# One step of a hybrid decoder on one core: the experts' weight fetches cut into runs of 2 and 4 KB, and the next block's rows copied behind the sigmoids

## The chip, the cores and the metric

The kernel runs on one NeuronCore of a Trainium2 chip. TensorE (PE) multiplies matrices, VectorE (DVE) and ScalarE (ACT) work on tiles, GpSimd (POOL) and SyncE (SP) issue most transfers, and 16 DMA engines move the bytes. The metric is the device time of one execution in microseconds (us), given as the median of several runs.

## What is computed

One layer for 2048 prompt tokens and 32 sample tokens: a modulated norm, one input projection, stick-breaking attention beside a gated linear recurrence, an output projection, and then a mixture of 32 experts, of which each token uses two. The last part is the one that matters here:

```python
def routed_experts(x, expert_idx, gate, w1, w3, w2):
    # pairs (token, expert) are sorted by expert into blocks, each block belonging to one expert
    def expert_block(args):
        toks, e = args
        xb = x_pad[toks]
        hb = jax.nn.silu(xb @ w1[e]) * (xb @ w3[e])
        return hb @ w2[e]
    out = lax.map(expert_block, (row_tok.reshape(n_blocks, EXPERT_BLOCK), block_expert))
    ...
```

w1 and w3 are 1024 x 512 and w2 is 512 x 1024, all float32, so an expert has three matrices of 2 MB. The token rows are 1024 numbers wide.

## The kernel before

The phases follow each other: modulation, projections, attention, the output projection with the router, the experts, and a final phase that gathers the experts' results, adds them and normalises. The change is in the experts (`experts_of`), with the matching layouts elsewhere.

The router writes each token row into `xs_d0` and `xs_d1` in memory, sorted by expert. The experts' phase then works through blocks of 64 rows; an expert has at least one block, and its number of blocks is read at run time (`n_blocks`), so that every engine runs a loop over an expert's blocks, 32 loops after each other. In this trace there are 80 blocks; by the times of the fetches of SP most experts have 2 or 3, and some have 1 or 4. A block has two units (u = 0, 1) of 32 rows.

Its steps, each on one engine, with the lines of the kernel:

- POOL (`load`, L1935) issues four transfers of 64 KB for the rows of a block into `x_in` (the profile shows `rowsP<-xs_d`), a double buffer, waits until they have landed, then issues two stores of 128 KB (`store`, L1944, `ys_d<-y`) of the result of two blocks earlier, and goes on with the next block's load. Both go by the software queue q0.
- ACT (`landed`, L1965) waits for the rows of block n + 1 and copies them into `x_turn` (shown as `o_rs<-rowsP`). It then does the sigmoids of block n (`gated`, L1970, `sg<-bank`), one for each unit, and last copies block n's result out of its bank (`result`, L1975, `y<-bank`).
- DVE multiplies the sigmoid with both products (L2033, L2035) and transposes the outcome into `hT` (L2037), for one unit; then it turns that unit of the next block's rows, `x_turn` into `xT` (`turn_rows`, L2028, shown as `o_sq<-o_rs`); then the same for the other unit.
- PE does the first products of both units (`hidden`, L1993, 64 matmuls each), which need `xT` and the expert's w1 and w3, and then the second products (`out`, L2000, 32 each), which need `hT` and w2. `xT` and the banks `h` have one buffer for each unit.
- SP fetches the weights by the hardware queue q1 into three slots: w1 and w3 of an expert (L1908) when the last block of the expert three before it has finished `hidden`, and w2 (L1916) when it has finished `out`. A transfer of 2 MB is laid out so that each of the 128 partitions gets one run of 16 KB.

The slots are memory of earlier phases (`oT`, `w_out`, `w`), which is why the profile shows the fetches as `oT<-in_w`, `w_out<-in_w` and `w<-in_w`. Waits are counted semaphores. On each engine instructions run in the order written.

Of the kernel before, what the change touches and what calls it, by code (L numbers as in the profile page):

```python
# [15 lines left out]
P = 128  # L16
D = 1024
KC = D // P
# [15 lines left out]
DE = D // 2  # L34
EC = DE // P
G = 64
STRIPS = 4
Q = P // STRIPS
UNITS = G // Q
# [806 lines left out]
def attention_phase(nc, io, keep, sems):  # L846
# [20 lines left out]
    for n in range(TICKS):  # L867
        unit, p = place(n)
# [15 lines left out]

    with ExitStack() as stack:
        k = Kit(nc, stack)
        shared = keep["w13_0"][:, :, :, :].rearrange("p a c n -> p (a c n)")
        kT = [shared[:, SEQ * i:SEQ * i + SEQ] for i in range(2)]
        qT = [shared[:, SEQ * (2 + i):SEQ * (2 + i) + SEQ] for i in range(2)]
        vv = [k.sb(f"vv{i}", [P, NT, P]) for i in range(2)]  # L890
# [532 lines left out]
def router(nc, io, keep, sems, k):  # L1423
# [59 lines left out]
    def sync(sp):  # L1483
        sp.dma_start(nf_row[:, :], io["norm_ffn"].to_broadcast([P, D])).then_inc(s["small"], 16)

        def load_x(i):
            if i == 0:
                sp.dma_start(x_t[0][0:NS, :], io["x_sample"].rearrange("b t n -> (b t) n")).then_inc(s_x[0], 16)
            else:
                sp.dma_start(x_t[i % 2][:, :], x_src[i - 1]).then_inc(s_x[i % 2], 16)  # L1490

        def load_rg(i):
            sp.dma_start(featT[i % 2][:, FC:, :], rgT[i - 1]).then_inc(s_rg[i % 2], 16)

        load_rg(1)
        load_x(0)
        sp.dma_start(w_r[:, :, 0:NG], io["w_group"][0].rearrange("(c p) n -> p c n", p=P)).then_inc(s["wr"], 16)
        sp.dma_start(w_r[:, :, 8:RW], io["w_router"][0].rearrange("(c p) n -> p c n", p=P)).then_inc(s["wr"], 16)
        sp.dma_start(b_r[:, 0:NG], io["b_group"].to_broadcast([P, NG])).then_inc(s["small"], 16)
        sp.dma_start(b_r[:, 8:RW], io["b_router"].to_broadcast([P, NE])).then_inc(s["small"], 16)  # L1500
        load_x(1)
        load_rg(2)
        for at, name in enumerate(("w1", "w3")):
            sp.dma_start(keep["w13_0"][:, at, :, :], io[name][0, 0].rearrange("(p c) n -> p c n", p=P)).then_inc(sems["pre"], 16)
        for i in range(NTL):
            sp.wait_ge(s["x1"], i + 1)
            sp.dma_start(io["x1_d"][row0[i]:row0[i] + size[i], :], x1[i % 2][0:size[i], :]).then_inc(s_st[i % 2], 16)
            if i + 2 < NTL:
                load_x(i + 2)
            if i >= 1 and i + 2 < NTL:  # L1510
                sp.wait_ge(s["mm1"], i + 1)
                load_rg(i + 2)
        for b in range(2):
            sp.wait_ge(s_st[b], 16 * len(range(b, NTL, 2)))
# [336 lines left out]
def experts_of(nc, io, keep, sems, k, emptied):  # L1851
# [37 lines left out]
    def sync(sp):  # L1889
        done = sp.alloc_register("blocks_done")  # L1890
        sp.reg_mov(done, 0)
        emptied(sp, "low")
        sp.dma_start(w2[0][:, :, :], src["w2"][0].rearrange("(p j) n -> p j n", p=P)).then_inc(s_w2[0], 16)
        sp.wait_ge(sems["placed"], 1)
        sp.wait_ge(s["in"], 64)
        for e in range(NE):
            i = e % SLOTS
            if e == 1:
                emptied(sp, "oT")
            if e == 2:  # L1900
                emptied(sp, "w_out")
            if e >= SLOTS:
                sp.reg_add(done, done, blocks_of(sp, e - SLOTS))
                freed = sp.snap(done, min_val=1, max_val=MAX_BLOCKS)
                hold(sp, s["h1"], freed, s["sp"])
            if e > 0:
                for at, name in enumerate(("w1", "w3")):
                    sp.dma_start(w13[i][:, at, :, :], src[name][e].rearrange("(p c) n -> p c n", p=P)).then_inc(s_w13[i], 16)  # L1908
            if e == 1:
                emptied(sp, "mid")  # L1910
            if e == 2:
                emptied(sp, "high")
            if e >= SLOTS:
                hold(sp, s["y"], freed, s["sp"])
            if e > 0:
                sp.dma_start(w2[i][:, :, :], src["w2"][e].rearrange("(p j) n -> p j n", p=P)).then_inc(s_w2[i], 16)  # L1916
        x1_rows = io["x1_d"][0:SEQ, :].rearrange("(t p) n -> p t n", p=P)
        sp.reg_add(done, done, blocks_of(sp, NE - 3))
        hold(sp, s["y"], sp.snap(done, min_val=1, max_val=MAX_BLOCKS), s["sp"])
        sp.dma_start(keep["x1_a"], x1_rows[:, 0:8, :]).then_inc(sems["x1_a"], 16)  # L1920
        sp.dma_start(keep["x1_b"], x1_rows[:, 8:12, :]).then_inc(sems["x1_b"], 16)
        sp.reg_add(done, done, blocks_of(sp, NE - 2))
        hold(sp, s["y"], sp.snap(done, min_val=1, max_val=MAX_BLOCKS), s["sp"])
        sp.dma_start(keep["x1_c"], x1_rows[:, 12:16, :]).then_inc(sems["x1_c"], 16)
        sp.dma_start(keep["x1_s"], io["x1_d"][SEQ:, :]).then_inc(sems["x1_s"], 16)
# [34 lines left out]
    def scalar(act):  # L1960
        def landed(n):

            act.wait_ge(s["in"], 64 * n + 64)
            act.wait_ge(s["xT"], 2 * n + 1)
            act.activation(x_turn[:, :].rearrange("p (u c a) -> p u c a", u=UNITS, c=KC),  # L1965
                           x_in[:, ds(n & 1, 1), :].rearrange("p z (u a c) -> p (z u) c a", u=UNITS, c=KC), ACT.Copy).then_inc(s["cp"], 1)

        def gated(n, u):
            act.wait_ge(s[f"h{u}"], n + 1)
            act.activation(sg[:, u, :], h[u][:, 0:P], ACT.Sigmoid).then_inc(s["sg"], 1)  # L1970

        def result(n):
            act.wait_ge(s["st"], 32 * n + 64)
            act.wait_ge(s["y"], n + 1)
            act.activation(y[:, ds(n & 1, 1), :].rearrange("p a n -> p (a n)"), yb[:, :], ACT.Copy).then_inc(s["ye"], 1)  # L1975

        def body(n, e, b, extra):
            landed(n + 1)
            for u in range(UNITS):
                gated(n, u)  # L1980
            result(n)

        act.nop().then_inc(s["xT"], 1)
        act.wait_ge(sems["placed"], 1)
        landed(0)
        experts(act, body)

    def tensor(pe):
        def hidden(i, u):

            for c in range(KC):
                for q in range(STRIPS):
                    mm = pe.matmul(h[u][q * Q:q * Q + Q, 0:2 * P], xT[:, c, u, :], w13[i][:, :, c, q * P:q * P + P], start=(c == 0), stop=(c == KC - 1))  # L1993
            return mm

        def out(i, u):

            for j in range(EC):
                for q in range(STRIPS):
                    mm = pe.matmul(yb[q * Q:q * Q + Q, u * (XW // 2):(u + 1) * (XW // 2)], hT[:, u, j, :], w2[i][:, j, q * (XW // 2):(q + 1) * (XW // 2)],  # L2000
                                   start=(j == 0), stop=(j == EC - 1))
            return mm

        def body(n, e, b, extra):
            i = e % SLOTS
            for u in range(UNITS):
                pe.wait_ge(s["xT"], 2 * n + u + 2)
                hidden(i, u).then_inc(s[f"h{u}"], 1)
            pe.wait_ge(s_w2[i], 16 * (e // SLOTS) + 16)
            for u in range(UNITS):  # L2010
                pe.wait_ge(s["hT"], 2 * n + u + 1)
                mm = out(i, u)
            mm.then_inc(s["y"], 1)

        def before(e):
            i = e % SLOTS
            if e == 0:
                pe.wait_ge(sems["pre"], 32)
            else:
                pe.wait_ge(s_w13[i], 32 * (e // SLOTS + (1 if i else 0)))  # L2020

        pe.wait_ge(sems["placed"], 1)
        experts(pe, body, before)

    def vector(dve):
# [4 lines left out]
        def body(n, e, b, extra):  # L2030
            for u in range(UNITS):
# [3 lines left out]
                dve.tensor_tensor(hid[:, u, :], sg[:, u, :], h[u][:, P:2 * P], ALU.mult)  # L2035
                dve.drain()
                dve.transpose(hT[:, u, :, :].rearrange("p j b -> p (j b)"), hid[:, u, :].rearrange("p (a j) -> p j a", j=EC)).then_inc(s["hT"], 1)  # L2037
                turn_rows(n + 1, u)

        for u in range(UNITS):  # L2040
# [158 lines left out]
def build_program(nc, io):  # L2199
    with ExitStack() as stack:  # L2200
# [35 lines left out]
        keep["rowsP"] = k.sb("rowsP", [P, 4, D])  # L2236
        rows_s = k.sb("rowsS", [P, 4, D])
        keep["rowsS"], keep["rows_mem"] = rows_s[0:NS, :, :], (keep["rowsP"], rows_s)
        keep["w13_0"] = k.sb("w13_0", [P, 2, KC, DE])
        keep["oT"], keep["w_out"] = k.sb("oT", [P, FC, SEQ]), k.sb("w_out", [P, 2, KC, 512])  # L2240
        for name in ("w_out0", "w_out1", "rows", "x1_a", "x1_b", "x1_c", "x1_s"):
            sems[name] = k.sem(name)
        attention_phase(nc, io, keep, sems)
        for i in range(3):
            keep[f"w2_{i}"] = k.sb(f"w2_{i}", [P, EC, D])
        keep["w13_1"] = keep["oT"][:, :, :].rearrange("p f n -> p (f n)").rearrange("p (a c n) -> p a c n", c=KC, a=2)
        keep["w13_2"] = keep["w_out"][:, :, :, :]
        tiles = lambda t: t[:, :, :, :].rearrange("p a c n -> p (a c n)").rearrange("p (t d) -> p t d", d=D)
        keep["x1_a"], keep["x1_b"] = tiles(keep["w13_2"]), keep["w2_2"][:, :, :]
        keep["x1_c"], keep["x1_s"] = tiles(keep["w13_0"])[:, 0:4, :], tiles(keep["w13_0"])[0:NS, 4, :]  # L2250
        keep["yy"] = tiles(keep["w13_1"])
# [35 lines left out]
```

## Time and profile before

| | |
|---|---|
| median of 3 runs | 3134.55 us (3132.65 to 3138.47) |
| the profiled execution, its own time | 3157.24 us |
| its span in the trace | 3155.8 us |
| PE busy | 2642.2 us, 84% of the span |
| DVE busy | 1365.3 us, 43% |
| ACT busy | 1051.0 us, 33% |
| POOL busy | 647.3 us, 21% |

Busy time counts the spans of instructions. In the experts' phase, from the first `hidden` at 1846.5 us to the end of the last `out` at 3058.9 us, PE is busy for less of the time than elsewhere. The profile page cuts the span into 40 slices of 79 us; the experts lie in slices 24 to 39. A row of the cost list gives the line, the engine, what it writes and reads and the shapes, how often, then busy time, the mean of one, and the idle time of the engine just before such instructions with what ended it.

### The profile page before, as it was taken

To read this page: it belongs to the slowest core of one execution; us is meant where nothing else is said; L and a number is where in the kernel's file an instruction comes from. 1 tells how busy PE (TensorE), PEld (TensorE's weight loads), DVE (VectorE), ACT (ScalarE), POOL (GpSimd) and SP (SyncE) were. 2 spreads that over 40 slices of the span, in tenths; PEclk is the share of its full clock that TensorE was granted. 3 is DMA by queue.
4 is the path that set the end of the run, shared out by engine and by line. 5 is a ranking of instruction groups with operands and counts; after the bars stand their busy time and mean duration, and the time that the engine had idled before them with its cause. 6 is when DMAs were issued, how large, how long until landed. Compare 5 with 4: busy or idle time off the path is not lost. (4 is left out here: it accounts for less than half of the span.)

```text
span 3155.8 us, 63798 instructions
## 1 busy us (share of the span) xinstructions
PE 2642.2 (84%) x23589; PEld 1368.9 (43%) x23589; DVE 1365.3 (43%) x2816; ACT 1051.0 (33%) x1942; POOL 647.3 (21%) x914
## 2 busy tenths in 40 slices
PE   7999999968898989999999927977678846777777
PEld 3444444424454444454355514544344423443443
DVE  2141424237787878888677721211111111111118
ACT  2313030216777777777222112111111111111114
POOL 0101010110121111111022222322232212222233
PEclk8999999988999999999999959988899878898889
DMA  8020201175776776767434365566455587656537
GB/s 300 13 80 15 78 27 67 49 258 179 264 252 225 238 235 228 247 223 240 157 126 144 120 244 194 191 208 240 152 198 174 165 294 245 237 156 246 186 107 305
DMA packets 225280, 576.76 MB, mean 183 GB/s; under 512 B 78230, under 2 KB 94679, under 8 KB 208780
## 3 DMA queue, kind: packets, MB, share of 16 engines
q1 hardware_dynamic: 123304, 427.99, 37.7%
q0 software_dynamic: 101440, 145.99, 15.4%
q8 instruction: 115, 1.88, 0.2%
q14 instruction: 97, 0.79, 0.1%
q10 hardware_dynamic: 324, 0.10, 0.0%
HBM read 460.86 MB, written 112.29 MB: 182 GB/s over the span
## 5 line engine op out<-in xcount | busy, mean ns | idle before, releaser
L2000 PE MATMUL bank<-w,hT 128*32 128x256 f32 x5120 | 348.2, 431 | 315.2 <-DVE hT L2037 315.2
L2033 DVE TENSOR_TENSOR sg<-sg,bank 128x128 f32<-128x128 f32 x160 | 44.6, 279 | 978.9 <-ACT sg L1970 978.7
L1253 DVE TENSOR_TENSOR_SCAN left<-leave,left 128x512 f32<-128x512 f32 (+3 forms) x320 | 358.4, 1120 | 135.9 <-ACT leave L1135 135.3
L2000 PEld LDWEIGHTS bank<-w,hT 128*32 128x32 f32 x5120 | 173.0, 124 | 483.3 <-DVE hT L2037 347.9
L442 PE MATMUL bank<-xnT,w_in 128*128 128x512 f32 x768 | 330.3, 592 | 0.0
L1944 POOL DMA_DIRECT2D ys_d<-y x164 | 115.9, 712 | 810.0 <-issue 743.6
L1056 POOL DMA_DIRECT2D w_out<-in_cache_v x256 | 137.8, 538 | 661.2 <-issue 656.0
L1965 ACT ACTIVATE o_rs<-rowsP 128x512 f32 (+1 forms) x81 | 92.9, 1146 | 464.6 <-DMA rowsP<-xs_d 454.2
L1935 POOL DMA_DIRECT2D rowsP<-xs_d x324 | 215.1, 672 | 85.1 <-issue 84.2
L1993 PE MATMUL bank<-w,o_sq 128*32 128x256 f32 x3840 | 214.7, 382 | 20.0 <-DVE o_sq L2028 20.0
L1620 PE MATMUL bank<-w_out,w 128*128 128x512 f32 x512 | 229.4, 601 | 2.5 <-DVE w L1684 2.5
L442 PEld LDWEIGHTS bank<-xnT,w_in 128*128 128x128 f32 x768 | 145.6, 190 | 181.8 <-issue 178.9
L442 PE MATMUL bank<-w_in,xnT 128*128 128x512 f32 x512 | 220.4, 592 | 0.0
L1137 ACT ACTIVATE take<-zb,biasP 128x512 f32<-128x512 f32 (+3 forms) x320 | 207.2, 647 | 0.0
L1135 ACT ACTIVATE leave<-zb,nbiasP 128x512 f32<-128x512 f32 (+3 forms) x320 | 204.5, 639 | 8.0 <-PE zb L1297 8.0
L1304 PE MATMUL tb<-ident,take 128*128 128x128 f32 x1088 | 182.4, 285 | 28.8 <-DVE take L1159 25.1
L1993 PE MATMUL bank<-oT,o_sq 128*32 128x256 f32 x3712 | 205.6, 379 | 0.5 <-issue 0.5
L1159 DVE TENSOR_TENSOR take<-take,left 128x512 f32<-128x512 f32 (+3 forms) x320 | 194.7, 609 | 15.5 <-DVE left L1253 0.4
L1291 PE MATMUL zb<-w 64*128 64x512 f32 (+3 forms) x640 | 164.3, 591 | 30.5 <-ACT take L1137 19.4
L1304 PEld LDWEIGHTS tb<-ident,take 128*128 128x128 f32 x1088 | 120.4, 143 | 147.0 <-issue 79.0
L1339 PE MATMUL tb<-ident,w_out 128*128 128x128 f32 x1024 | 160.7, 281 | 27.4 <-DMA w_out<-in_cache_k 22.4
L1975 ACT ACTIVATE y<-bank 128x512 f32 x80 | 47.8, 597 | 387.2 <-PE bank L2000 337.4
(409 smaller groups left out, 3424.9 us busy)
## 6 DMA issues: line engine op xcount, KB each, us to landing
w<-in_w SPq DMA_DIRECT2D x54, 2048.0 KB, 15.9
w_out<-in_cache_v POOLq DMA_DIRECT2D x256, 256.0 KB
w_out<-in_cache_k SPq DMA_DIRECT2D x256, 256.0 KB
oT<-in_w SPq DMA_DIRECT2D x22, 2048.0 KB, 14.1
w_out<-in_w SPq DMA_DIRECT2D x20, 2048.0 KB, 14.4
ys_d<-zeros SPq DMA_DIRECT2D x32, 816.0 KB
ys_d<-y POOLq DMA_DIRECT2D x166, 128.0 KB, 4.8
rowsP<-xs_d POOLq DMA_DIRECT2D x324, 64.0 KB, 4.0
```

The source lines that it names most:

```text
L442: mm = pe.matmul(ps[:, :], w, m, start=(i == 0), stop=(i == len(parts) - 1))
L1135: act.activation(leave[n % 4][:, 0:cols], zb[n % 3][:, 0:cols], ACT.Sigmoid, scale=-SCALE, bias=keep["nbiasP"][:, head:head + 1]).then_inc ...
L1137: act.activation(take[n % 4][:, 0:cols], zb[n % 3][:, 0:cols], ACT.Sigmoid, scale=SCALE, bias=keep["biasP"][:, head:head + 1]).then_inc(s_ ...
L1159: dve.tensor_tensor(take[n % 4][:, 0:cols], take[n % 4][:, 0:cols], left[n % 4][:, 1:cols + 1], ALU.mult).then_inc(s_w, 1)
L1253: dve.tensor_tensor_scan(left[n % 4][:, 0:cols][:, ::-1], leave[n % 4][:, 0:cols][:, ::-1], leave[n % 4][:, 0:cols][:, ::-1], left[n % 4][ ...
L1291: mm = pe.matmul(zb[(n + par) % 3][:, 0:cols], qT[pair % 2][half, t * P:t * P + P], kT[pair % 2][half, c * GRP:c * GRP + cols], start=True ...
L1304: mm = pe.transpose(to[:, j * P:j * P + P], take[n % 4][:, j * P:j * P + P], ident[:, :])
L1339: mm = pe.transpose(to[:, i * P:i * P + P], kp[g % 2][:, i, f * P:f * P + P], ident[:, :])
L1620: mm = pe.matmul(pb[half][0:n, :], lhs, w_out[:, half, c, :], start=(c == 0), stop=(c == KC - 1))
L1935: pool.dma_start(x_in[64 * half:64 * half + 64, ds(n & 1, 1), u * (XW // 2):(u + 1) * (XW // 2)].rearrange("p a n -> p (a n)"), in_strips( ...
L1993: mm = pe.matmul(h[u][q * Q:q * Q + Q, 0:2 * P], xT[:, c, u, :], w13[i][:, :, c, q * P:q * P + P], start=(c == 0), stop=(c == KC - 1))
L2000: mm = pe.matmul(yb[q * Q:q * Q + Q, u * (XW // 2):(u + 1) * (XW // 2)], hT[:, u, j, :], w2[i][:, j, q * (XW // 2):(q + 1) * (XW // 2)], s ...
```

## The change

The layout of the w1/w3 slots goes from [w1 or w3, c, n] to [c, w1 or w3, n], c being the 8 rows of the matrix that a partition holds. The transfer of one matrix therefore writes 8 runs of 2 KB into a partition, in place of one of 16 KB; in memory it is still 16 KB in one piece. PE reads the two halves of its operand 2 KB apart in place of 16 KB. The fetch of w2 is cut into four transfers, one for each j, with 4 KB for each partition, and the wait of PE counts four times as much. On ACT the wait for the next block's rows and their copy come after both sigmoids. On DVE both units' products come first, and then both turns.

```diff
@@ experts, sync
-                    sp.dma_start(w13[i][:, at, :, :], src[name][e].rearrange("(p c) n -> p c n", p=P)).then_inc(s_w13[i], 16)
+                    sp.dma_start(w13[i][:, :, at, :], src[name][e].rearrange("(p c) n -> p c n", p=P)).then_inc(s_w13[i], 16)
...
-                sp.dma_start(w2[i][:, :, :], src["w2"][e].rearrange("(p j) n -> p j n", p=P)).then_inc(s_w2[i], 16)
+                for j in range(EC):
+                    sp.dma_start(w2[i][:, j, :], src["w2"][e].rearrange("(p j) n -> j p n", p=P)[j]).then_inc(s_w2[i], 16)
@@ experts, scalar
         def body(n, e, b, extra):
-            landed(n + 1)
             for u in range(UNITS):
                 gated(n, u)
+            landed(n + 1)
             result(n)
@@ experts, tensor
-                    mm = pe.matmul(h[u][q * Q:q * Q + Q, 0:2 * P], xT[:, c, u, :], w13[i][:, :, c, q * P:q * P + P], start=(c == 0), stop=(c == KC - 1))
+                    mm = pe.matmul(h[u][q * Q:q * Q + Q, 0:2 * P], xT[:, c, u, :], w13[i][:, c, :, q * P:q * P + P], start=(c == 0), stop=(c == KC - 1))
...
-            pe.wait_ge(s_w2[i], 16 * (e // SLOTS) + 16)
+            pe.wait_ge(s_w2[i], 16 * EC * (e // SLOTS + 1))
@@ experts, vector
                 dve.transpose(hT[:, u, :, :].rearrange("p j b -> p (j b)"), hid[:, u, :].rearrange("p (a j) -> p j a", j=EC)).then_inc(s["hT"], 1)
+            for u in range(UNITS):
                 turn_rows(n + 1, u)
```

The first expert's w1 and w3, fetched in the router's phase (L1504), and its w2 (L1893) are cut in the same way, and the views of this memory in the attention and the final phase are renamed to match, at the same addresses.

On ScalarE, in the loop of the second expert, one block is this before (`o_rs<-rowsP` is the copy of the next block's rows, `sg` the two sigmoids, `y` the result; an ISA row is a wait or a count):

```order
L1884 ISA
L1964 ISA
L1965 REGISTER_ALU
L1965 ISA
L1965 ACTIVATE o_rs<-rowsP 128x512
L1970 ACTIVATE sg<-bank_4 128x128
L1970 ACTIVATE sg<-bank_6 128x128
L1973 ISA
L1975 REGISTER_ALU
L1975 ISA
L1975 ACTIVATE y<-bank_3 128x512
```

and this with the change:

```order
L1884 ISA
L1972 ACTIVATE sg<-bank_4 128x128
L1972 ACTIVATE sg<-bank_6 128x128
L1965 ISA
L1966 ISA
L1967 REGISTER_ALU
L1967 ISA
L1967 ACTIVATE o_rs<-rowsP 128x512
L1975 ISA
L1977 REGISTER_ALU
L1977 ISA
L1977 ACTIVATE y<-bank_3 128x512
```

The copy and its two waits stand behind both sigmoids now, and still ahead of the result.

On VectorE one block of the first expert is this before (`hT` feeds PE's second products, `o_sq` is one unit of the next block's rows turned):

```order
L2033 TENSOR_TENSOR sg<-sg,bank_4 128x128
L2035 TENSOR_TENSOR hid<-sg,bank_4 128x128
L2037 STREAM_TRANSPOSE hT<-hid 128x128
L2027 REGISTER_ALU
L2028 STREAM_TRANSPOSE o_sq<-o_rs 128x8x32
L2032 REGISTER_ALU
L2033 TENSOR_TENSOR sg<-sg,bank_6 128x128
L2035 TENSOR_TENSOR hid<-sg,bank_6 128x128
L2037 STREAM_TRANSPOSE hT<-hid 128x128
L2028 STREAM_TRANSPOSE o_sq<-o_rs 128x8x32
```

and this with the change:

```order
L2035 TENSOR_TENSOR sg<-sg,bank_4 128x128
L2037 TENSOR_TENSOR hid<-sg,bank_4 128x128
L2039 STREAM_TRANSPOSE hT<-hid 128x128
L2034 REGISTER_ALU
L2035 TENSOR_TENSOR sg<-sg,bank_6 128x128
L2037 TENSOR_TENSOR hid<-sg,bank_6 128x128
L2039 STREAM_TRANSPOSE hT<-hid 128x128
L2029 REGISTER_ALU
L2030 STREAM_TRANSPOSE o_sq<-o_rs 128x8x32 x2
```

The first turn moved behind the second unit's `hT`, and both turns stand together at the end of the block.

On SyncE the fetches of one later expert are this before (w1 and w3, then w2):

```order
L1874 TENSOR_LOAD n_blocks
L1874 ISA x2
L1903 ISA
L1908 DMA w_0<-in_w 128x4096 x2
L1916 DMA w_0<-in_w 128x4096
```

and this with the change:

```order
L1874 TENSOR_LOAD n_blocks
L1874 ISA x2
L1904 ISA
L1909 DMA w_0<-in_w 128x8x512 x2
L1918 DMA w_0<-in_w 128x1024 x4
```

The order of the fetches is the same; w2 has four instructions in place of one.

## Rows read from the trace of the kernel before

**Rows 1.** The experts' whole phase: start:end, its length, each engine's busy time.

```profile
1846.50:3058.90 1212.40, 896.36 (x15360) 498.39 (x15360) 206.49 (x641) 184.43 (x328) 326.29 (x482) 0.87 0.60 204
```

**Rows 2.** The page's cost list: the experts' instructions, busy, mean ns, idle before.

```profile
L2000 PE MATMUL bank<-w,hT 128*32 128x256 f32 x5120 | 348.2, 431 | 315.2 <-DVE hT L2037 315.2
L1965 ACT ACTIVATE o_rs<-rowsP 128x512 f32 (+1 forms) x81 | 92.9, 1146 | 464.6 <-DMA rowsP<-xs_d 454.2
```

**Rows 3.** Who waited for whom from 1900 us on: us in total, times, longest.

```profile
PE bank L2000 <- DVE hT L2037: 281.8, 37, 24.5
```

**Rows 4.** Timeline of ACT, PE, POOL and SP around one weight fetch.

```profile
2257.70 1.12 ACT L1965 ACTIVATE o_rs<-rowsP 128x512 f32 x1 [18.11 <-DMA rowsP<-xs_d]
2258.72 0.43 ACT L1970 ACTIVATE sg<-bank 128x128 f32<-128x128 f32 x2
...
2238.52 7.09 PE L1993 MATMUL bank<-oT,o_sq 128*32 128x256 f32 x128
...
2234.66 2.65 POOL L1935 DMA_DIRECT2D rowsP<-xs_d  x4 [0.52 <-issue]
2258.50 1.41 POOL L1944 DMA_DIRECT2D ys_d<-y  x2 [21.19 <-issue]
...
2235.32 0.81 SPq L1908 DMA_DIRECT2D w<-in_w  x2
2238.83 0.33 SPq L1916 DMA_DIRECT2D w<-in_w  x1
```

**Rows 5.** Timeline of PE, ACT, POOL and DVE in blocks with no fetch running.

```profile
2265.41 7.08 PE L1993 MATMUL bank<-oT,o_sq 128*32 128x256 f32 x128
2272.32 3.69 PE L2000 MATMUL bank<-w,hT 128*32 128x256 f32 x64
2275.82 7.09 PE L1993 MATMUL bank<-oT,o_sq 128*32 128x256 f32 x128
...
2277.13 1.16 ACT L1965 ACTIVATE o_rs<-rowsP 128x512 f32 x1 [0.23 <-DMA rowsP<-xs_d]
2282.98 0.28 ACT L1970 ACTIVATE sg<-bank 128x128 f32<-128x128 f32 x1 [3.17 <-PE bank L1993]
...
2270.20 2.65 POOL L1935 DMA_DIRECT2D rowsP<-xs_d  x4 [0.52 <-issue]
...
2284.01 0.42 DVE L2037 STREAM_TRANSPOSE hT<-hid 128x128 f32<-128x128 f32 x1
2284.36 0.40 DVE L2028 STREAM_TRANSPOSE o_sq<-o_rs 128x256 f32<-128x256 f32 x1
```

**Rows 6.** DMA packets by queue: a fetch running (2240:2252), none (2266:2292), attention (848:856).

```profile
q1 hardware_dynamic: 296, 4.33, 95.7%
q0 software_dynamic: 287, 0.14, 4.4%
...
q0 software_dynamic: 1959, 1.27, 21.6%
...
q0 software_dynamic: 463, 1.51, 51.6%
q1 hardware_dynamic: 762, 1.40, 47.8%
```

**Rows 7.** Stretches with 2 KB runs alone (35:50) and weight fetches; last: DMA share, GB/s.

```profile
35.00:40.00 5.00, 3.02 (x20) 1.64 (x12) 2.08 (x5) 0.00 (x0) 0.00 (x0) 0.50 1.05 387
...
2300.00:2306.00 6.00, 3.77 (x75) 2.00 (x68) 1.06 (x4) 1.46 (x3) 1.41 (x2) 1.00 1.02 419
...
2244.00:2250.00 6.00, 1.61 (x32) 0.70 (x24) 0.00 (x0) 0.00 (x0) 0.00 (x0) 1.00 1.02 362
```

**Rows 8.** Issue durations of SP's 2 MB transfers in 2 KB runs: ns min/median/max.

```profile
L152 SPq DMA_DIRECT2D w_in<-in_w_in x3: 1183/5021/21543, 7.3 to 30.1; - x3
```

**Rows 9.** SP's fetches where experts have a single block each.

```profile
2578.03 0.81 SPq L1908 DMA_DIRECT2D w<-in_w  x2
...
2614.23 1.08 SPq L1908 DMA_DIRECT2D oT<-in_w  x2
```

More of the change, by code:

```diff
@@ L886, in attention_phase @@
         k = Kit(nc, stack)
-        shared = keep["w13_0"][:, :, :, :].rearrange("p a c n -> p (a c n)")
+        shared = keep["w13_0"][:, :, :, :].rearrange("p c a n -> p (c a n)")
         kT = [shared[:, SEQ * i:SEQ * i + SEQ] for i in range(2)]
@@ L1503, in sync @@
         for at, name in enumerate(("w1", "w3")):
-            sp.dma_start(keep["w13_0"][:, at, :, :], io[name][0, 0].rearrange("(p c) n -> p c n", p=P)).then_inc(sems["pre"], 16)
+            sp.dma_start(keep["w13_0"][:, :, at, :], io[name][0, 0].rearrange("(p c) n -> p c n", p=P)).then_inc(sems["pre"], 16)
         for i in range(NTL):
@@ L1892, in sync @@
         emptied(sp, "low")
-        sp.dma_start(w2[0][:, :, :], src["w2"][0].rearrange("(p j) n -> p j n", p=P)).then_inc(s_w2[0], 16)
+        for j in range(EC):
+            sp.dma_start(w2[0][:, j, :], src["w2"][0].rearrange("(p j) n -> j p n", p=P)[j]).then_inc(s_w2[0], 16)
         sp.wait_ge(sems["placed"], 1)
@@ L1915, in sync @@
             if e > 0:
-                sp.dma_start(w2[i][:, :, :], src["w2"][e].rearrange("(p j) n -> p j n", p=P)).then_inc(s_w2[i], 16)
+                for j in range(EC):
+                    sp.dma_start(w2[i][:, j, :], src["w2"][e].rearrange("(p j) n -> j p n", p=P)[j]).then_inc(s_w2[i], 16)
         x1_rows = io["x1_d"][0:SEQ, :].rearrange("(t p) n -> p t n", p=P)
@@ L2238, in build_program @@
         keep["rowsS"], keep["rows_mem"] = rows_s[0:NS, :, :], (keep["rowsP"], rows_s)
-        keep["w13_0"] = k.sb("w13_0", [P, 2, KC, DE])
+        keep["w13_0"] = k.sb("w13_0", [P, KC, 2, DE])
         keep["oT"], keep["w_out"] = k.sb("oT", [P, FC, SEQ]), k.sb("w_out", [P, 2, KC, 512])
@@ L2245, in build_program @@
             keep[f"w2_{i}"] = k.sb(f"w2_{i}", [P, EC, D])
-        keep["w13_1"] = keep["oT"][:, :, :].rearrange("p f n -> p (f n)").rearrange("p (a c n) -> p a c n", c=KC, a=2)
-        keep["w13_2"] = keep["w_out"][:, :, :, :]
-        tiles = lambda t: t[:, :, :, :].rearrange("p a c n -> p (a c n)").rearrange("p (t d) -> p t d", d=D)
+        keep["w13_1"] = keep["oT"][:, :, :].rearrange("p f n -> p (f n)").rearrange("p (c a n) -> p c a n", c=KC, a=2)
+        keep["w13_2"] = keep["w_out"][:, :, :, :].rearrange("p h c n -> p (h c n)").rearrange("p (c a n) -> p c a n", c=KC, a=2)
+        tiles = lambda t: t[:, :, :, :].rearrange("p c a n -> p c (a n)")
         keep["x1_a"], keep["x1_b"] = tiles(keep["w13_2"]), keep["w2_2"][:, :, :]
```

## The prediction

> **What bounds the kernel now.** The window over the experts' phase comes first, since every edit lies there: 1212.4 us, in which PE is busy for 896 us at a granted clock of 0.87, with the DMA engines at 0.60 [rows 1]. So neither is full. The cost list then says what PE waits for: its second products (L2000) stand idle for 315.2 us, all of it on `hT` from DVE, and take 348.2 us themselves [rows 2]. The list of waits counts 37 such waits from 1900 us on, up to 24.5 us long [rows 3]. In the same list ACT's copy of the next block's rows idles for 464.6 us until the rows have landed [rows 2].
>
> The timeline around one fetch joins the two [rows 4]. SP issues w1 and w3 at 2235.3 and w2 at 2238.8. POOL issues the rows of the next block at 2234.7 to 2237.3, and ACT can copy them only at 2257.7. PE ended its first products at 2245.6, and both sigmoids, which need nothing but these, run at 2258.7, because they stand behind the copy. In blocks with no fetch running PE never stops: first products from 2265.41 and again from 2275.82, a period of 10.42 us; the copy starts 1.3 us after the start of a block and is done before the first of PE's two units is ready, half of 7.09 us in [rows 5]. So the bound is a chain: **rows held behind weights, then sigmoids held behind rows, then PE**. 80 blocks (5120 matmuls of 64 each, [rows 2]) at 10.42 us are 834 us; the other 378 us are this chain and its cold clock: 315.2 us idle, and 348.2 - 80 x 3.69 = 53 us of second products that run slow after a halt [rows 2, 5].
>
> **The change: the runs of 2 and 4 KB.** The turn behind a weight packet shrinks. 2 KB runs alone moved 387 GB/s over 16 engines, so one takes 2.048 x 16 / 387 = 0.085 us [rows 7]; a 4 KB one is twice that, 0.17 us. How many go by in one turn is not shown for these two transfers. The nearest row is the attention phase, K in 2 KB runs on q1 beside V in 4 KB packets on q0: 762 packets to 463, 1.65 to one, about equal bytes [rows 6]. So a block's 49 packets cost 49 x 0.085 = 4.2 us at one run a turn, 6.9 us at 1.65, 8.3 us beside w2. Without a fetch, the loads go from the start of issue (2270.20) to the copy (2277.13) in 6.9 us, of which 2.65 is issuing and most is latency; the packets run beside that [rows 5]. I add to the landing, inside a fetch: 0.5 us at the best, 5 us at the worst (all turns of 4 KB and none beside the issuing), and take **2.9 us**, nearest to the attention row.
>
> The Trainium skill (DMA: Bandwidth & Descriptors, SWDGE vs HWDGE vs iDMA) calls a packet the point at which an engine switches queues, and prefers at most 4096 B for one. Turns of 4 KB would be 0.17 us for both matrices, the upper half of my range; the 14.6 KB mean of [rows 6] shows that packets are larger where a run is.
>
> The fetch itself hardly slows: 387 GB/s against 362 to 419 with 16 KB runs [rows 7], 6.29 MB in 16.3 us. SP's issue of a 2 KB-run transfer can block for 1.2 to 21.5 us [rows 8]; behind it on SP stand only the later fetches (and the loads of x1 at the end), in their order anyway, so I cost it at nothing; were the DMA engines idle meanwhile, it would be the rival on weights below. Three more issues for w2 at 0.33 us each [rows 4] lie on SP too. PE's operand with halves 2 KB apart has no row of its own; the matmuls run the same from all slots, so nothing.
>
> **The change: the order.** In the block above PE can do its second products (3.69 us, with 1.2 us of DVE's steps ahead, 2283.26 to 2284.43 [rows 5]) while it waits for the rows. Before, rows had to land within 2.5 us of a block's start to hold nobody (the copy of 1.16 us must end when the first unit does, at 3.6 us). With the change they must land 2.0 us before the next block (copy 1.16, turn 0.40, steps between), at 8.4 us. They land at 1.1 to 1.3 us [rows 5], so slack grows from 1.3 to about 7 us. The late turns cost nothing: the second sigmoid is at 2282.98, 7.2 us into its block, the copy then ends at 8.4, DVE's products by 8.6, both turns by 9.5, and PE needs them at 10.42 [rows 5]. If they were late, each block would pay the difference, 1 us for 80.
>
> **What is late next: POOL's own loop.** It loads, waits for the landing, stores, loads. Copy at 2257.70 (rows landed just before), the next issue 2.7 us later (stores 0.8 us after the copy's start, 1.41 us long, 0.52 us to the next issue [rows 4]), 2.65 issuing, about 4 to land: 9.4 us a turn, only 1 us less than PE's 10.42. Inside a fetch it is 9.4 + 2.9 = 12.3 us. 32 fetches of 16.3 us are 522 us, 59% of a phase near 890 us. Mean turn 9.4 + 0.59 x 2.9 = **11.1 us**, above 10.42: the rows' loop sets the pace, by a little. Then 80 x 11.1 = 888, and 2.5 us for the cold first block: 891 us against 1212.4, a gain of 321. From the profiled 3157.2 that leaves 2836; that execution stands 22.7 us over the median of 3134.55, so I forecast **2813 us**.
>
> Its ends: if the extra landing is 0.5 us, PE sets the pace, 80 x 10.42 + 2.5 = 836, gain 376, 2758 us. If it is 5 us, the loop is 9.4 + 0.55 x 5 = 12.2, the phase 975, gain 237, 2897 us.
>
> **The rivals.** *Rows still wait for the whole fetch.* The DMA engines might take turns by more than one short run, or join the runs of w1 and w3, whose 16 KB stand in one piece in memory. Against it stands the 1.65 to one of attention [rows 6]. Then only the order helps: the 37 waits [rows 3] lose up to 4.9 us each, I take 4, 148 us, and the fetches are longer by some 0.6 us, 20 in all: 3157 - 128 - 22.7 = 3006 us. By the Trainium skill (DMA: Bandwidth & Descriptors, Queues, rings and completion order) an engine drains a whole packet of typically 9 to 17 descriptors before it switches rings. With 2 KB runs that would be a turn as long as before or longer, and this rival; rows 6 show 1.65 in attention, not 9. Chance 12%.
>
> *PE waits for weights.* At the faster pace an expert of one block gives 10.4 us for a fetch of 16.3; fetches at 2578.0 and 2614.2 follow one block each [rows 9]. Three slots cover two such in a row. Should 2 KB runs beside rows move only 240 GB/s, a fetch takes 26 us, and four or five short experts cost 15 us each, with other small gaps: about 100 us more, 2915 us. Attention's window, 2.91 MB in 8 us on both queues, 364 GB/s, speaks against it [rows 6]. Chance 8%.
>
> *Slower.* The same mechanism, worse: SP's blocked issues [rows 8] let q1 run dry between runs. It decides from where a fetch takes longer than an expert does now, 1212.4 / 32 = 37.9 us, that is under 166 GB/s. At 150 GB/s, 41.9 us and 1341 us in all, 3263 us. 387 GB/s behind blocked issues at 35 us speaks against it [rows 7]. Chance 3%.
>
> **The numbers.** Forecast 75% (2758 to 2897), rows still held 12% (2960 to 3050), weights 8% (2880 to 3100), slower 3%, no change 2%. The range 2755 to 2940 holds the first and half the weights' case, 8 in 10. A difference under 0.2% can't be told from none here. Faster 0.95, same 0.02, slower 0.03.
>
> **What would show it.** Right: idle of L2000 on `hT` falls from 315 us to under 30, L2000's mean from 431 to about 380 ns, the clock above 0.95; what idle is left stands before L1993, on `o_sq` from DVE, behind ACT's copy behind the rows; the rows' longest landing falls from beyond 20 us to near 10; q1's packets rise by some 70,000. Wrong: ACT's copy still starts at the end of fetches (the first rival); PE's first products idle on a transfer of `in_w` (the second); fewer GB/s while a fetch runs alone (the third).

## The result, and the profile after

| | before | changed |
|---|---|---|
| median | 3134.84 us (3132.65 to 3138.47, 4 runs) | 3005.06 us (3003.26 to 3017.72, 4 runs) |
| ratio to before | | 0.9594, 95% interval 0.9566 to 0.9621 |
| span of the profiled execution | 3155.8 us | 3001.8 us |
| experts' phase | 1212.4 us | 1060.7 us |

The kernel is faster by 130 us, where 321 were forecast and at least 195 within the range. All of the gain is in the experts' phase: from the end of the last `out` to the end of the kernel it is 97 us in both. The phase is shorter by 152 us and not by 130, because the profiled execution of the kernel before ran 22 us over its median and that of the changed kernel 2 us under; all readings of the traces below carry this. The window over the phase, to be held against [rows 1]:

```profile
1844.50:2905.20 1060.70, 900.43 (x15360) 500.21 (x15360) 221.66 (x641) 184.12 (x323) 325.49 (x482) 0.93 0.77 233
```

PE's wait has changed its place. The cost list of the changed kernel, against [rows 2] (the second products are L2002 here, the first L1995, by the slot they read):

```profile
L1995 PE MATMUL bank<-w,o_sq 128*32 128x256 f32 x3840 | 238.9, 412 | 86.8 <-DVE o_sq L2030 86.8
L2002 PE MATMUL bank<-w,hT 128*32 128x256 f32 x5120 | 295.8, 381 | 0.0
L1995 PE MATMUL bank<-oT,o_sq 128*32 128x256 f32 x3712 | 221.8, 400 | 48.0 <-DVE o_sq L2030 45.5
L1995 PE MATMUL bank<-w_out,o_sq 128*32 128x256 f32 x2688 | 164.4, 407 | 45.2 <-DVE o_sq L2030 43.8
```

The idle of 315.2 us ahead of the second products is gone, and 86.8 + 48.0 + 45.2 = 180 us stand ahead of the first ones, on the turned rows. The cold clock went there with it: second products run at 381 ns, and the first ones take 625 us in place of 80 x 7.09 = 567. Around one such halt, of 3.8 us in the timeline below, the granted clock (PEclk, the third number from the end) is 1.00 before it and 0.60 behind it:

```profile
2238.00:2242.00 4.00, 3.97 (x75) 1.98 (x64) 1.00 (x3) 0.28 (x1) 0.00 (x0) 1.00 1.10 262
2245.70:2250.00 4.30, 4.26 (x48) 2.29 (x52) 0.31 (x1) 0.00 (x0) 2.24 (x4) 0.60 1.01 389
```

So the phase would be 834 + 180 + 58 = 1072 us; it is 1060.7, as parts of these overlap. The waits beneath, from 1890 us on:

```profile
ACT o_rs L1967 <- DMA rowsP<-xs_d: 217.0, 49, 9.1
PE bank L1995 <- DVE o_sq L2030: 149.3, 38, 7.6
```

So ACT still waits for rows, 49 times, but never for more than 9.1 us. The timeline around one fetch shows how late, POOL first, then ACT, PE and SP:

```profile
2230.85 2.65 POOL L1937 DMA_DIRECT2D rowsP<-xs_d  x4 [0.55 <-issue]
2244.89 1.41 POOL L1946 DMA_DIRECT2D ys_d<-y  x2 [11.40 <-issue]
...
2238.52 0.28 ACT L1972 ACTIVATE sg<-bank 128x128 f32<-128x128 f32 x1 [3.18 <-PE bank L1995]
2244.09 1.12 ACT L1967 ACTIVATE o_rs<-rowsP 128x512 f32 x1 [5.29 <-DMA rowsP<-xs_d]
...
2238.27 3.70 PE L2002 MATMUL bank<-w,hT 128*32 128x256 f32 x64
2245.74 4.48 PE L1995 MATMUL bank<-w_out,o_sq 128*32 128x256 f32 x48 [3.77 <-DVE o_sq L2030]
...
2228.16 1.29 SPq L1909 DMA_DIRECT2D oT<-in_w  x2
2231.67 6.12 SPq L1918 DMA_DIRECT2D w<-in_w  x4
```

The fetch starts at 2228.2, and its last piece lands at 2253.0. The rows issued at 2230.8 are copied at 2244.1, 13.2 us later and well before the fetch is over; in [rows 4] it took 23.0 us, the whole fetch. SP's four issues of w2 take 6.1 us, held one after the other.

**The mean turn of POOL's loop** tells all the kernels of this study apart. A load is the time from the first of a block's row transfers' issue to the last one's landing; the gap is the time from there to the next block's issue. Both are means over the 80 blocks, worked out from the issues and landings in the traces (the profile's own rows show single transfers, so that these means have no row).

| | load | of them over 10 us | gap | load + gap | phase / 80 |
|---|---|---|---|---|---|
| before | 11.3 us | 35, mean 17.3 | 3.8 us | 15.1 us | 15.2 us |
| changed | 9.5 | 36, mean 13.1 | 3.7 | 13.2 | 13.3 |
| short runs alone | 10.0 | 44, mean 12.5 | 3.7 | 13.6 | 13.7 |
| new order alone | 12.0 | 29, mean 21.9 | 3.7 | 15.7 | 15.7 |
| rows in wide transfers | 8.6 | 33, mean 11.5 | 3.5 | 12.1 | 12.3 |
| stores issued ahead | 10.4 | 50, mean 12.5 | 2.0 | 12.4 | 12.5 |

In every one of them the phase is 80 turns of this loop, to within 0.2 us a turn. That alone proves nothing, since any loop that keeps step with the blocks has this length. What shows that this one sets the pace is that POOL waits in it for nothing but its own landings. When nothing else holds it, its first store follows the landing by 1.07 us. In the changed kernel that is so, to 0.15 us, in 78 of 80 turns, and all 80 lose 1 us together on anything else; in the kernel before it is 68 of 80, and 7.5 us together. **So POOL's loop set the pace already in the kernel before**, and PE's 315 us on `hT` were what it left idle. The gap's 3.7 us are 1.07 us, 1.41 us of stores (more in some turns) and 0.5 to 0.6 us to the next load; in 31 turns, as many as there are changes of expert, that last step takes 1.1 us more.

### The profile page after: what moved, and what is told of

It is laid out like the page before. It is cut to its first block and busy times, and to the rows that moved or that the text cites. A ratio compares the mean times of both kernels' runs of the same rounds, so it can differ in the third digit from the quotient of the medians.

```text
span 3001.8 us, 63970 instructions
## 1 busy us (share of the span) xinstructions
PE 2644.7 (88%) x23589; PEld 1370.9 (46%) x23589; DVE 1380.3 (46%) x2816; ACT 1051.2 (35%) x1938; POOL 647.7 (22%) x914
## 3 DMA queue, kind: packets, MB, share of 16 engines
q0 software_dynamic: 101440, 145.99, 16.0%
## 5 line engine op out<-in xcount | busy, mean ns | idle before, releaser
L1995 PE MATMUL bank<-w,o_sq 128*32 128x256 f32 x3840 | 238.9, 412 | 86.8 <-DVE o_sq L2030 86.8
L2002 PE MATMUL bank<-w,hT 128*32 128x256 f32 x5120 | 295.8, 381 | 0.0
L1995 PE MATMUL bank<-oT,o_sq 128*32 128x256 f32 x3712 | 221.8, 400 | 48.0 <-DVE o_sq L2030 45.5
L1972 ACT ACTIVATE sg<-bank 128x128 f32<-128x128 f32 x160 | 44.4, 278 | 567.7 <-PE bank L1995 567.7
L1995 PEld LDWEIGHTS bank<-w,o_sq 128*32 128x32 f32 x3840 | 129.6, 119 | 193.6 <-DVE o_sq L2030 95.1
L2002 PEld LDWEIGHTS bank<-w,hT 128*32 128x32 f32 x5120 | 157.1, 110 | 124.2 <-DVE hT L2039 26.8
L1995 PE MATMUL bank<-w_out,o_sq 128*32 128x256 f32 x2688 | 164.4, 407 | 45.2 <-DVE o_sq L2030 43.8
L1995 PEld LDWEIGHTS bank<-oT,o_sq 128*32 128x32 f32 x3712 | 123.4, 115 | 144.0 <-DVE o_sq L2030 52.3
## 6 DMA issues: line engine op xcount, KB each, us to landing
w<-in_w SPq DMA_DIRECT2D x128, 512.0 KB, 15.1
```

## The experiments

Experiments 1 to 4, 5 to 8 and 9 to 12 ran in three groups, each beside executions of the kernel before, with medians of 3139.9, 3131.9 and 3140.0 us; the changed kernel's own comparison had 3134.8. Ratios are to these. A difference in us between kernels of different groups is good to some 8 us, and where it matters, the one by the ratios stands beside it.

**1. The short runs alone**: the changed kernel with ACT's and DVE's order of before.

```diff
         def body(n, e, b, extra):
+            landed(n + 1)
             for u in range(UNITS):
                 gated(n, u)
-            landed(n + 1)
             result(n)
```

> The short runs alone, with the order of the kernel before: the copy still stands ahead of both sigmoids. The theory now (the turns of the rows' packets were priced too low: beside 2 KB runs a block's rows take about 13 us from issue to landing in place of the 8 to 10 forecast, so that POOL's loop of load, landing, store makes about 16 us inside a fetch): that loop sets the pace whatever ACT's order is, so 3005 to 3050 us, with the rows' longest landing near 13 us. The first rival of the prediction (only the order helps, the rows still wait for the whole fetch): 3135 to 3155 us and landings of 20 us and more.

Measured: 3047.7 us, ratio 0.9702 (0.9639 to 0.9766), the longest landing of a row transfer 14.5 us. The loop holds, and the first rival of the prediction, by which the short runs change nothing for the rows, is out. The time lies at the upper end of the first range. The idle time is back at its old place, 189.6 us:

```profile
L2002 PE MATMUL bank<-w,hT 128*32 128x256 f32 x5120 | 354.4, 438 | 189.6 <-DVE hT L2039 189.6
```

**2. The new order alone**: the kernel before, with the diff's lines on ACT and DVE and nothing else.

> The new order on ACT and DVE alone, with runs of 16 KB. The prediction priced this at 3134.8 - 148 = 2987 us, fetches staying as they are. The theory now expects the same, 2980 to 3010 us, with rows landing only at the end of a fetch (over 20 us) and PE's waits moved from the second products to the first. If the short runs carry the gain and the order nothing, 3110 to 3135 us.

Measured: 3202.5 us, ratio 1.0175 (1.0115 to 1.0236), slower than before by 1.2 to 2.4%. It lies in neither range: the prediction's price for the order and the theory as it stood both failed. The timeline of this kernel, POOL, SP and PE:

```profile
2220.75 2.64 POOL L1935 DMA_DIRECT2D rowsP<-xs_d  x4 [0.63 <-issue]
...
2255.05 2.65 POOL L1935 DMA_DIRECT2D rowsP<-xs_d  x4 [0.52 <-issue]
...
2218.57 0.81 SPq L1908 DMA_DIRECT2D w_out<-in_w  x2
...
2252.65 0.80 SPq L1908 DMA_DIRECT2D w<-in_w  x2
...
2228.69 3.69 PE L2000 MATMUL bank<-w,hT 128*32 128x256 f32 x64
2242.80 9.72 PE L1993 MATMUL bank<-w,o_sq 128*32 128x256 f32 x128 [10.42 <-DVE o_sq L2028]
```

POOL's load of 2220.75 stands behind the fetch of 2218.57, and PE waits for it until 2242.80. It has done its second products during the wait, as it should. But SP asks for the next weights as soon as the first products that follow are done (2242.80 + 9.72 = 2252.52), at 2252.65, and POOL's load of 2255.05 falls right behind that and waits for the whole fetch. In the old order PE has its second products still to do when the rows land, some 5 us, and the request comes that much later. The traces bear this out over the 29 fetches of w1 and w3 for which they have both landings. In the new order the next load is issued 0.6 to 4.4 us behind 26 of them, and takes 18.9 to 33.9 us. In the kernel before only 4 have a load that close behind; 19 have one 0.3 to 3.1 us ahead, and 12 of these 19 loads landed in under 20 us, the shortest in 10.4. Loads of over 20 us number 20 here and 11 before. The idle time ahead of the first products is 371 us:

```profile
L1993 PE MATMUL bank<-w,o_sq 128*32 128x256 f32 x3840 | 235.8, 408 | 148.9 <-DVE o_sq L2028 148.0
L1993 PE MATMUL bank<-oT,o_sq 128*32 128x256 f32 x3712 | 228.8, 409 | 113.3 <-DVE o_sq L2028 113.3
L1993 PE MATMUL bank<-w_out,o_sq 128*32 128x256 f32 x2688 | 170.1, 417 | 109.1 <-DVE o_sq L2028 108.9
```

**3. Fewer packets for the rows**: the changed kernel, with whole rows in one array.

```diff
                 for u in range(UNITS):
-                for half in range(2):
-                    pool.dma_start(x_in[64 * half:64 * half + 64, ...], in_strips(io[f"xs_d{half}"], row, u))
+                pool.dma_start(x_in[:, ...], in_strips(io["xs_d"], row, u))
```

> The changed kernel, with the two arrays of half rows made one array of whole rows (room for 2048 rows for each expert), so that a block's rows come in two transfers of 128 partitions and 128 KB in place of four of 64 partitions and 64 KB, as the stores of results do, which show no 16-byte packets. The theory (40 of a block's 49 packets for each engine are 16-byte ones, each takes a turn of about 0.16 us beside the fetch): if the tiny packets go with the 64-partition form, a load lands within 8 us inside a fetch, PE sets the pace again and the time is 2790 to 2850 us. If the tiny packets stay, 2980 to 3010 us. If bytes and not packets hold the rows, no change, 2990 to 3010 us with the tiny packets gone.

Measured: 2929.9 us, ratio 0.9319 (0.9263 to 0.9374), between the cases. The tiny packets did not go, and the premise was wrong: stores have them too. Two stores stand alone in 3050 to 3060 us of the kernel before, with 64 packets of 4 KB for their 256 KB, and 224 under 512 B:

```profile
q0 software_dynamic: 288, 0.27, 11.8%
```

By size the trace has 192 packets of 16 B among them, 96 for each store, and 32 of 4 B. Over the whole kernel that leaves 112 for each load of 64 KB and, in this experiment, 96 for each load of 128 KB. A block has 54 packets on each engine, 36 of its loads and 18 of its stores; with the wide transfers the loads too have 18. So q0's packets fall by a quarter (the changed kernel has 101440):

```profile
q0 software_dynamic: 77568, 145.64, 16.0%
```

The bytes are the same, and inside a fetch a load takes 11.5 us in place of 13.1. Most of that is not the contention, though: with no fetch beside it a load takes 5.3 us in place of 6.3, since POOL issues two transfers in place of four (1.4 us in place of 2.65). What a fetch adds falls only from 6.8 to 6.2 us, with the loads' packets halved. The mean turn falls by 1.1 us, and the fewer issues alone take 1.0 off a quiet load. At a fixed 0.16 us a packet, 18 fewer on each engine would have taken 2.9 us off a load inside a fetch; so the packets do not set the landing alone.

**4. The stores out of the loop**: the changed kernel, in which POOL issues a block's loads, then the stores, and then waits for the landing.

```diff
-            hold(pool, s["in"], 64 * n + 64, s["sp"])
...
             store(n)
+            hold(pool, s["in"], 64 * n + 64, s["sp"])
```

> The changed kernel, but POOL issues the stores of an earlier result right behind a block's loads and waits for their landing only then, so that the stores no longer lie between a landing and the next issue. The theory (POOL's loop sets the pace): a turn inside a fetch falls from about 16 to about 13.5 us, 60 of 80 blocks gain some 2 us, 2870 to 2930 us. If PE or the weights set the pace: no change, 3000 us.

Measured: 2942.4 us, ratio 0.9355 (0.9298 to 0.9411). That is a gain, but 12 us short of the range. The gap fell by 1.7 us; loads rose by 0.9, which the expectation had left out (the stores' packets may now run among theirs). This is a gain of 63 us over the changed kernel (75 by the ratios) by an edit that touches no transfer, and the plainest sign that the loop sets the pace.

**5. No fetches**: experts 4 to 32 use the weights of the first three.

> The changed kernel without the fetches of the 4th to the 32nd expert: these compute with the weights of the first three. It leaves 29 x 6.29 MB of transfers out and shows the phase with nothing beside the rows. The theory (rows lose time only to the fetch; quiet, a load takes 6.3 us and the next issue 3.7 more, under PE's 10.42): the experts' phase takes 80 x 10.42 and some 15 us for the start, about 850 us, and the whole 2785 to 2805 us. If POOL's loop is the bound even when quiet, 2830 us and more.

Measured: 2803.9 us, one run, phase 859 us. This is the floor of PE's pace. Quiet, load and gap are 6.3 + 3.7 = 10.0 us, just under PE's 10.42. Here POOL does wait for others: its first store follows the landing by over 1.2 us in 36 of 80 turns, 23 us together.

**6. w2 by one transfer** of 16 KB runs, the rest as changed.

> The changed kernel with w2 fetched by one transfer of 16 KB runs again; w1 and w3 keep 2 KB. The theory (one turn of the rows' queue is one run of the weights' queue): rows that meet the w2 part of a fetch, 8 turns of 0.65 us for each engine in place of 32 of some 0.2 us, land later by 3 to 5 us; with one block in two to three meeting it, 3040 to 3110 us. If the runs of w2 don't matter, 2995 to 3015 us.

Measured: 3010.3 us, ratio 0.9594 (0.9553 to 0.9636). No difference from the changed kernel, against the expectation. Loads of the rows are asked for right after w1 and w3 and meet those. The expectation had taken the fetch for evenly spread over the rows. The cut of w2 is worth nothing here.

**7. Runs of 1 KB** for w1 and w3.

> The changed kernel with w1 and w3 in runs of 1 KB (w2 stays at 4 KB). In the changed kernel a turn of a rows' packet beside 2 KB runs takes 0.16 us. If about 0.085 of it is the run and the rest is fixed, a turn falls to 0.11 to 0.12 us, a load inside a fetch from 13.1 to about 11 us, and half the blocks gain 2 us: 2900 to 2960 us. If the turn is a cost of the rows' own packet, whatever stands beside it, landings stay at 13 us, fetches get longer, and the time is 3005 to 3050 us.

Measured: 2993.6 us, ratio 0.9552 (0.9511 to 0.9594), some 11 us under the changed kernel, so neither case in full; the intervals of the two ratios touch, and the phase in the traces is 10 us shorter (1050.7 us). Packets by queue in a stretch where rows and weights share the engines, first the changed kernel (2236 to 2240 us), then this one (2229 to 2233):

```profile
q1 hardware_dynamic: 403, 0.80, 81.0%
q0 software_dynamic: 402, 0.27, 29.2%
```

```profile
q1 hardware_dynamic: 617, 0.62, 86.1%
q0 software_dynamic: 450, 0.19, 36.4%
```

402 packets of the rows in 4 us on 16 engines are one in 0.159 us; with 1 KB runs 450 are one in 0.142 us. Halving the run takes 0.017 us off the turn, not 0.04. But it is no longer one run a turn: 617 to 450 is 1.37, so that a turn still carries 1.4 KB of weights. By estimate from 0.085 us for 2 KB, the runs' part of a turn falls from 0.085 to 0.058 us, and the rest, 0.074 and 0.084 us, stays. In the kernel before a turn was 12 x 16 / 287 = 0.67 us [rows 6].

**8. Wide rows and stores ahead together**, on the changed kernel.

> Rows in two transfers of 128 partitions (room for 2048 rows for each expert) and the stores of results issued ahead of the wait for the landing, both on the changed kernel. Alone they gave loads of 8.6 us and 3.5 us to the next issue, and 10.4 and 2.0 us. The theory (the phase is 80 turns of POOL's loop, a turn being load and gap, with PE's 10.42 below it): 8.6 + 1.0 for the later stores + 1.8 = 11.4 us, 912 us of phase, 2855 to 2885 us. If the gains overlap, 2915 to 2930 us.

Measured: 2833.6 us (2832.3 to 2836.5), ratio 0.9039 (0.9004 to 0.9075), 21 us under the range and 30 us above the run without fetches. Loads 8.7, gap 2.4, 11.1 us a turn, and a phase of 895 us, 11.2 a block. For the first time something else shows beside the loop, 16 us on the weights:

```profile
L1994 PE MATMUL bank<-w,o_sq 128*32 128x256 f32 x3840 | 215.8, 383 | 34.7 <-DVE o_sq L2029 25.1 <-DMA w<-in_w 9.5
L1994 PE MATMUL bank<-w_out,o_sq 128*32 128x256 f32 x2688 | 153.6, 387 | 14.8 <-DVE o_sq L2029 7.9 <-DMA w_out<-in_w 6.2 <-issue 0.8
```

This version gives each expert room for 2048 rows less the first 64, which is enough for these inputs and not for every routing. Experiment 4 has no such limit.

**9 and 10. What each half of the change is worth once the loop is fast.** Number 9 is number 8 with runs of 16 KB, number 10 is number 8 with the old order.

> The kernel of e8_wide_ahead (rows in two wide transfers, room for 2048 rows for each expert, stores ahead of the wait) with the weights in runs of 16 KB again, in the new order. The theory: a load's 36 packets for each engine are still more than a fetch's 24, so rows are held for whole fetches, about 20 us, and only the shorter gap (2.3 in place of 3.7 us) and quiet load (5.3 in place of 6.3 us) help: a loop of 13 to 13.8 us, 2960 to 3040 us. If the short runs owe their gain only to the slow loop, it is within 1% of e8's 2833.6 us.

> The kernel of e8_wide_ahead with ACT's and DVE's order of the kernel before (the copy ahead of both sigmoids). The theory: where POOL's loop no longer sets the pace, the slack that the new order gives (about 6 us a block) is what hides a late load; without it each load that lands over 2.5 us into its block is paid at once. 27 loads over 10 us, 2 to 3 us each: 2880 to 2930 us. If the order is worth nothing here either, 2830 to 2845 us.

Measured: 2980.9 us (ratio 0.9478, 0.9430 to 0.9526) and 2876.8 us (0.9150, 0.9103 to 0.9196). The first is in its range, the second 3 us under it. So the runs are worth 147 us there (138 by the ratios), and the order 43 us (35 by the ratios). In number 10 the idle is ahead of the second products again:

```profile
L2001 PE MATMUL bank<-w,hT 128*32 128x256 f32 x5120 | 306.1, 392 | 67.4 <-DVE hT L2038 67.1
```

**11. Runs of 1 KB on number 8.**

> The kernel of e8_wide_ahead with w1 and w3 in runs of 1 KB. On the changed kernel this gave 11 us (loads inside a fetch 11.8 in place of 13.1 us, fetches slower). Here little is left above the floor of 2804 us: 2820 to 2835 us. If the slower fetch makes PE wait for weights, 2840 to 2870 us with idle of PE's first products on transfers of in_w.

Measured: 2842.8 us, ratio 0.9039 (0.8992 to 0.9087), the same as number 8 within the intervals. The time lies in the second case, and its sign came too: PE's idle on transfers of `in_w` is 24 us in place of 16. Finer runs have nothing left to give.

**12. Rows from a fixed address**, to see where the 16-byte packets come from.

```diff
-            load(n, pool.snap(e * CAP + offs + b * G))
+            load(n, e * CAP)
```

> The changed kernel with each block's rows read from a fixed place of its expert's room (rows of zeros), in place of an address from a register: the experts' results are those of zero rows, the transfers have the same size. It asks where the 16-byte packets come from. If from the register's address, q0's packets fall by some 50,000 and a load inside a fetch takes 6 to 8 us, phase about 860 us, 2800 to 2830 us. If they come from elsewhere (the destination, the shape), nothing changes: 2990 to 3015 us.

Measured: 2993.0 us, one run, and q0 has exactly as many packets as before:

```profile
q0 software_dynamic: 101440, 145.99, 16.1%
```

They do not come from the register's address in memory. The destination has one too (the half of the double buffer), and that was not tried here. But two stores to `ys_d` ahead of the phase (L1549 of the kernel before, issued at 1834.3 and 1835.1 us) have fixed addresses on both sides and 192 such packets all the same, and POOL's loads of V in the attention, whose address in memory comes from a register, have none. So an address from a register is not what brings them; where they come from stays open.

## Why the prediction was wrong

**The bound** was read right in part. Rows are held behind weights, and POOL's loop sets the pace of the changed kernel. But it was not "next" in line: it set the pace before as well, as its turns show, and the chain through the sigmoids into PE hung on it. That is why sigmoids ahead of the copy free PE's second products and yet give nothing by themselves. The signs it named came: no idle left on `hT` (0.0 us), second products at 381 ns, the idle on `o_sq` from DVE, 71168 more packets on q1. The clock (0.93, not above 0.95) and the longest landing (14.8 us for one transfer, not near 10) did not.

**The term that failed is the extra landing inside a fetch**, put at 2.9 us and at 5 us at the worst. It is 13.1 - 6.3 = 6.8 us, outside the range of its own bounds. Two errors make it. First, the price of a turn: 0.085 us for one 2 KB run, or 0.14 by the attention's 1.65 to one. The count of runs is in fact one (403 to 402), the lower end, but such a turn takes 0.159 us, more than the run alone: in the same stretch the engines moved 267 GB/s, against 377 in 2242 to 2244, when the rows were through.

```profile
2236.00:2240.00 4.00, 4.00 (x80) 2.23 (x72) 1.45 (x5) 0.28 (x1) 0.00 (x0) 1.00 1.10 267
...
2242.00:2244.00 2.00, 0.00 (x0) 0.00 (x0) 0.00 (x0) 0.00 (x0) 0.00 (x0) 1.00 1.03 377
```

The price of a run was taken from a stretch with one queue alone [rows 7], and counts of packets in the attention phase [rows 6] say nothing of the time of a turn. Second, the packets were thought to run beside the issuing and the latency, which is how the worst case came to 5 us where all 49 turns behind 4 KB are 8.3 by the prediction's own price. They stand behind the latency. The load issued at 2230.85 shows it: q0 moved 23 packets in 2231 to 2234, 713 in 2234 to 2242, 45 on each engine, and 6 in the 2 us after that; the load landed at 2243.8.

```profile
q0 software_dynamic: 23, 0.07, 5.9%
...
q0 software_dynamic: 713, 0.40, 22.4%
...
q0 software_dynamic: 6, 0.00, 0.4%
```

The 49 were no count of a load alone either, but of loads and stores; the loads of a block have 36 on each engine, and here the store before them, which landed at 2237.8, ran among them. How much of the 6.8 us is turns and how much the rest is not settled: experiment 3 halved the loads' packets and took only 0.6 us off.

The Trainium skill (DMA: Bandwidth & Descriptors, Queues, rings and completion order) has an engine drain 9 to 17 descriptors of a queue before it switches. No stretch here shows that; 403 to 402, and 296 to 287 in [rows 6], are one for one. Its other figure (same page, SWDGE vs HWDGE vs iDMA), packets of at most 4096 B, would allow two runs of 2 KB a turn; the trace shows one (with runs of 1 KB, 1.37 in the stretch of experiment 7).

**The gap** was put at 2.7 us from copy to issue, and 9.4 us for the quiet loop. Measured from the landing it is 3.7 us, and the quiet loop 6.3 + 3.7 = 10.0 us. That is 0.6 us x 80 = 48 us, some 35 of them the 1.1 us more in 31 turns, named above.

**The fetch** was put at 16.3 us for 6.29 MB, from a stretch without rows. What slows the rows slows the weights too: w1 and w3 alone take 20.0 us on average from issue to landing (17.1 before), the one above 24.8 us with w2. The sum with the measured terms, made after the fact: 10.0 + 36 / 80 x 6.8 = 13.1 us, and 80 x 13.1 = 1048 us of 1060.7, against the 888 that were forecast.

**The order** was said to give slack for nothing lost. The slack is there, but where POOL's loop sets the pace it buys nothing; what the order does is move the requests for the weights against the loads of the rows. With 16 KB runs that costs 63 us (experiment 2). With 2 KB runs it gains 43 us (3047.7 against 3005.1; 34 by the ratios): the gap is the same 3.7 us, but 36 loads in place of 44 take over 10 us. With the fast loop it gains as much (2876.8 against 2833.6); there the gap is 2.9 us in number 10 and 2.4 in number 8, against 2.0 in experiment 4, so that POOL waits for others at times and the slack may count. The two halves are no sum: against the 3139.9 us of before in that comparison the runs alone take 92 us off and the order alone adds 63, and together they take 130 us off.

**The first rival** gave 3006 us, and the kernel takes 3005. That is luck, and the rival is refuted: its mechanism, rows that still wait for the whole fetch and an order that saves 148 us, would have shown in experiments 1 and 2, which came out at 3047.7 and 3202.5 in place of 3135 to 3155 and 2987. Of the other rivals, PE's waits for weights are no row of the changed kernel's cost list; and SP's held issues [rows 8] were met, up to 10 us each, with no wait of PE for weights behind them.

## What to carry to other kernels

Where small transfers that an engine waits for share the DMA engines with a bulk fetch, look at the runs of the fetch, and not at its bytes: each packet of the small transfers waited for about one run of the large one, at 0.67 us with runs of 16 KB and 0.16 with runs of 2 KB. Price such a turn from a stretch where both queues are at work, and look for fewer issues and for a shorter loop around the wait before finer runs. To find which loop sets the pace, compare no sums, which agree for every loop that keeps step, but look for the one that waits for nothing but its own steps. An order that lets an engine run ahead also moves every request that hangs on it; write down what the earlier request will collide with before you book the slack.

## What the runs showed of the hardware

- A turn between the two queues took 0.159 us for a 2 KB run and a mostly 16-byte packet, where 2 KB alone take 0.085 us; the engines' throughput falls from 377 to 267 GB/s.
- A row transfer of 64 KB by POOL brings 112 packets of 16 B with it (7 on each engine), one of 128 KB 96, loads and stores alike. They stay with a fixed address in memory, and two stores with both addresses fixed have them.
- The issue of a transfer in short runs holds SP's queue, up to 10.4 us for one here, where no 16 KB-run transfer of the kernel before took over 0.9 us:

```profile
L1909 SPq DMA_DIRECT2D w_out<-in_w x20: 555/612/10397, 1852.5 to 2726.2; - x20
```
